# Every front-half step comes to ScalarE and VectorE one slot later than to TensorE

## The chip, the cores and the metric

The kernel runs on one core of one Trainium2 chip. The metric is device microseconds of that core for one execution of the whole program, the median of several runs. Its engines are TensorE (PE), VectorE (DVE), ScalarE (ACT), GpSimd (POOL) and the DMA queues that SyncE (SP) and POOL issue to. Each engine runs its own instruction list in order, and semaphores tie the lists together.

## The reference

One layer of a hybrid encoder is computed for 1024 prompt tokens and 64 tokens that continue a cached stream. Cut to what matters here:

```
h = rmsnorm(x)
p = h @ W_in                         # one input projection for all branches
A = gated linear attention (4 heads, blocks of 64 tokens)
B = forgetting attention (8 heads, 128 queries at a time, past of 512 for the stream)
M = cross attention into 256 memory tokens (4 heads)
x = x + W_out( sum_b sigmoid(G_b(h)) * (W_br[b] branch_b) )
h2 = rmsnorm(x)
# channel mixer: 8 heads, each picks 16 of 16384 single-neuron experts per token
for head in 8:
    e, w = top16 of product keys(h2, head)
    x += sum_e w_e * gelu(h2 . u_e) * v_e
```

## The kernel before

**Tiles and groups.** The tokens are cut into nine tiles of 128 (the last has the 64 tokens of the stream), and the tiles into four groups: tile 0, tiles 1 and 2, tiles 3 to 5, tiles 6 to 8. A group goes through a *front half*, and then its tiles go through the *experts*.

**Front half.** It is a list of steps: `in_prep` (norm and transposes), `in_unit` (a 451-column chunk of the input projection of one tile), `mix`, `fox` and `past` (the three branches, tile by tile; called mixers below; `past` prepares the caches), `gate` (gates and branch projections of the group), `out` (output projection, residual, second norm) and `sco` (scores for the picking of experts). A step has parts on several engines, which wait for one another: in a `fox` step PE makes scores in PSUM (L1151), VectorE adds the bias and takes the maximum (L1641, L1642), ScalarE exponentiates, PE transposes (L1166), ScalarE or VectorE copies (L1392, L1648), and PE multiplies by the values (L1179).

**Experts.** A token's expert is one 8 KB row that holds u_e and v_e. GpSimd gathers such rows by indirect DMA (L1847), one row for each of the 128 tokens, into a slot of a ring of eight. Two gathers make a *pair*; there are 544 pairs. For a pair VectorE makes two dot products (L1768), ScalarE the gelu and the weights and a diagonal matrix (`weigh`: L1448, L1451, L1456), and PE multiplies the diagonal with the v half (`pair`, L1284). For tiles 0 to 5 VectorE takes the second of the two value products from PE (L1784); the row for pair n stands behind the dots of pair n+1. On each head's first four pairs VectorE also does a piece of the picking of the next head's experts. The ring holds four pairs. GpSimd gathers three pairs ahead, and the gather of pair n+4 waits until PE's product of pair n and VectorE's of pair n are done.

**The order.** `make_plan` spreads the front steps of the next group over the pairs of this one. Its answer, PLAN, is a list of slots, each with one expert pair and the front steps beside it; the first group's front half stands alone at the start, the last group's pairs alone at the end. PE and SP go through a slot with `walk`: front steps first, then the pair. GpSimd gathers once a slot. ScalarE and VectorE use `trail`: the pair first, then what is left over from the slot before, then the steps of this slot. Before the change `trail` leaves `in_unit`, `gate` and `sco` steps over for the next slot, where they come behind the next pair, and does `in_prep`, `mix`, `fox`, `past` and `out` in their own slot.

Of the kernel before, what the change touches and what calls it, by code (L numbers as in the profile page):

```python
# [478 lines left out]
def layer(nc, c, t_in, outs, dram, ctx):  # L479
# [16 lines left out]
    def flat(at, n, parts=128):  # L496
        assert at + n <= AREA
        return c.area[:parts, at:at + n]
# [55 lines left out]
    sco = [flat(A0 + 7680 + k * 512, 512) for k in range(3)]  # L554
# [117 lines left out]
    def trail(front, experts):  # L672


        left = []
        for expert, beside in PLAN:
            if expert and expert[0] in experts:
                experts[expert[0]](*expert[1:])
            for step in left:
                front[step[0]](*step[1:])  # L680
            left = []
            for step in beside:
                if step[0] in ("in_unit", "gate", "sco") and expert:
                    left.append(step)
                elif step[0] in front:
                    for old in left:
                        front[old[0]](*old[1:])
                    left = []
                    front[step[0]](*step[1:])

    def walk(front, experts, front_first):
# [602 lines left out]
    def _(act):  # L1294
# [167 lines left out]
        def pair(i, r, q):  # L1462
# [7 lines left out]
            if piece == 2:  # L1470
                soften(head)

        trail({"in_prep": in_prep, "in_unit": in_unit_, "mix": mix, "fox": fox,
               "past": past, "gate": gate, "out": out_, "sco": sco_}, {"start": start, "pair": pair})


    @block.vector
    def _(dve):
# [341 lines left out]
        def end():  # L1820
            finish(NT - 1)

        trail({"in_prep": in_prep, "in_unit": in_unit_, "mix": mix, "fox": fox,
               "past": past, "gate": gate, "out": out_, "sco": sco_}, {"start": start, "pair": pair, "end": end})

# [120 lines left out]
```

How the kernel before makes its waits and increments, by code:

```python
            def step(ins):  # L210
                n[0] += 1
                ins.then_inc(s, 1)
                pool.wait_ge(s, n[0])
# [84 lines left out]
        @block.sync  # L298
# [4 lines left out]
            def mem(k):  # L303
# [11 lines left out]
                                        (c.go_bc[:, :], t_in["gla_g_out"], GDV), (c.bf_bc[:, :], t_in["fox_b_f"], FH),  # L315
                                        (c.gq_bc[:, :], t_in["fox_g_q"], FD), (c.gk_bc[:, :], t_in["fox_g_k"], FD),
                                        (c.gm_bc[:, :], t_in["mem_g_q"], MD)):
                        sp.dma_start(dst, src if n is None else src[0:1, :].broadcast_to([128, n])).then_inc(s_par, 16)
                if k == 3:
                    sp.wait_ge(s_kn, MT)
                    sp.dma_start(outs["mem_k"].rearrange("(a p) n -> p a n", p=128), kn[:, :, :]).then_inc(s_put, 16)
                    sp.wait_ge(s_mv, MT)
# [2 lines left out]
            def store(k):  # L325
                sp.wait_ge(s_ev[k % 2], k // 2 + 1)
                dst = rw_sp[k // 4].rearrange("p (a b) -> p a b", a=DT)
                sp.dma_start(dst[:, :, (k % 4) * 128:(k % 4 + 1) * 128], rw[k % 4][:, :, :]).then_inc(s_rw[k % 4], 16)
# [1 line left out]
            def route(k):  # L330
                if k:
                    if k + 3 < 16:
                        sp.wait_ge(s_mm, k)
                        load(k + 3)
                    store(k - 1)
            walk(mem, route)
            store(15)
            sp.wait_ge(s_mkT, 1)
            sp.dma_start(mkT_sp[:, :], mkT[:, :]).then_inc(s_put, 16)
            for k in range(4):
```

## Time and profile before

| what | value |
|---|---|
| runs | 4433.03, 4438.22, 4452.79 us, median 4438.22 us |
| the profiled execution | 4445.82 us, its span 4444.1 us |
| granted TensorE clock, mean | 0.875 |
| busy PE, DVE, ACT, POOL | 76%, 63%, 36%, 27% of the span |
| HBM traffic | 334 GB/s over the span |
| front half of group 0, alone | 0 to 424 us |
| mixers of fronts 1, 2, 3 beside pairs | 543 to 735, 1321 to 1668, 2467 to 3005 us |
| gates of fronts 2, 3 | 1668 to 1935, 3005 to 3286 us |
| pairs of group 3, alone | 3603 to 4444 us |

The span runs from the first to the last instruction; the profiled execution has 1.7 us around it, and lies 7.6 us over the median. Three fronts run beside pairs, and have to be looked at stage by stage: in some stages the DMA share is near 1, in others far below.

### The profile page before, as it was taken

Reading aid. Unit: us, or ns where it says so; the run is one execution under the profiler, and the core shown is the slowest. Engines: PE = TensorE matmul, PEld = TensorE weight load, DVE = VectorE, ACT = ScalarE, POOL = GpSimd, SP = SyncE. Lnnn points to the kernel's source line nnn. Section 1 sums busy time; section 2 is a strip of 40 time slices with the busy share of each in tenths; the row PEclk is TensorE's granted clock in tenths of the full one; section 3 lists DMA queues with packets and bytes.
Section 4 is the critical chain, followed back from the end, with each engine's and each line's share of the span. In section 5 each row is a group of like instructions: output and inputs, shape, how many; then the busy total and the mean of one; then the engine's idle time right before and its main releaser. Section 6 shows DMA issues by size and latency. Waiting matters only on the chain.

```text
span 4444.1 us, 33979 instructions
## 1 busy us (share of the span) xinstructions
PE 3389.7 (76%) x10219; PEld 1759.7 (40%) x10219; DVE 2805.9 (63%) x6048; ACT 1582.2 (36%) x3679; POOL 1216.8 (27%) x1122
## 2 busy tenths in 40 slices
PE   5765965986896776989689777576978867777777
PEld 4462444842444443544234344233543322322222
DVE  1112454547656784646777788685767886676677
ACT  1111154422315563432232455253443233333333
POOL 0000211113221222322333232242323344444443
PEclk9787976997997788999889778778989989999989
DMA  7557865889996788879999897878989999999998
GB/s 239 189 200 270 333 215 196 321 319 387 364 351 238 257 306 325 339 291 352 402 387 422 310 362 283 295 285 356 413 351 370 403 414 421 418 415 421 402 373 371
DMA packets 298492, 1484.95 MB, mean 334 GB/s; under 512 B 42740, under 2 KB 112372, under 8 KB 147716
## 3 DMA queue, kind: packets, MB, share of 16 engines
q0 software_dynamic: 156672, 1140.92, 64.7%
q1 hardware_dynamic: 141636, 341.86, 21.2%
q8 instruction: 81, 1.33, 0.1%
q14 instruction: 103, 0.84, 0.0%
HBM read 1415.59 MB, written 67.08 MB: 334 GB/s over the span
## 4 chain that ended last, share of the span: by engine, by line
PE 40%; DMA 24%; DVE 18%; ACT 6%; issue 6%; POOL 2%; SPq 1%; POOLq 0%; DVEq 0%; ACTq 0%
DMA c_ring<-in_uv,l_idx 17%; PE c_p_y L1284 11%; DVE c_ring L1768 7%; PE c_PB L1016 4%; PE c_PC L1016 4%; DVE l_ysb L1784 3%; PE c_PA L1271 2%; PE c_PA L1226 2%; PE c_PB L1271 2%; PE c_PB L1226 2%; PE c_PC L1226 2%; DMA c_area<-oT_sp 2%; POOL c_ring L1847 2%; PE c_PA L1254 1%; DMA c_area<-in_w_out 1%
## 5 line engine op out<-in xcount | busy, mean ns | idle before, releaser
L1847 POOL DMA_INDIRECT c_ring<-in_uv,l_idx x1088 | 1210.0, 1112 | 3203.8 <-PE c_p_y L1284 1400.0
L1284 PE MATMUL c_p_y<-c_ring,l_diag 128*128 128x512 f32 (+1 forms) x2816 | 1510.5, 676 | 451.5 <-ACT l_diag L1456 444.3
L1768 DVE CUSTOM_DVE_ANT_0 c_ring<-c_ring,l_h_cur 128x1024 f32<-128x1024 f32 x1088 | 1302.8, 1221 | 365.1 <-DMA c_ring<-in_uv,l_idx 356.6
L1284 PEld LDWEIGHTS c_p_y<-c_ring,l_diag 128*128 128x128 f32 (+1 forms) x2816 | 551.0, 207 | 1237.6 <-ACT l_diag L1456 650.9
L1448 ACT ACTIVATE l_gel<-l_dots 128x2 f32<-128x2 f32 x544 | 110.7, 203 | 1606.2 <-DVE l_dots L1768 1604.9
L1784 DVE SCALAR_TENSOR_TENSOR l_ysb<-c_ring,l_wgt,l_ysb 128x1024 f32<-128x1024 f32 x384 | 492.4, 1282 | 0.0
L1448 ACT ACT_TABLE_LOAD x207 | 265.6, 1283 | 60.0 <-DVE l_dots L1768 56.6
L1451 ACT ACTIVATE l_wgt<-l_gel,l_gw 128x1 f32<-128x1 f32 x1088 | 261.2, 287 | 17.9
L1456 ACT ACTIVATE l_diag<-c_ident,l_wgt 128x128 f32<-128x128 f32 x640 | 243.1, 399 | 16.7
L1016 PE MATMUL c_PB<-c_area 128*128 128x451 f32 (+1 forms) x576 | 228.4, 550 | 1.9 <-ACT c_area L1317 1.2
L1016 PE MATMUL c_PC<-c_area 128*128 128x451 f32 (+1 forms) x576 | 226.4, 546 | 4.3 <-DMA c_area<-in_w_in 4.3
L1226 PE MATMUL c_PA<-c_area 128*128 128x128 f32 (+3 forms) x512 | 132.1, 415 | 115.8 <-DMA c_area<-oT_sp 113.5
L1016 PEld LDWEIGHTS c_PB<-c_area 128*128 128x128 f32 (+1 forms) x576 | 107.1, 187 | 122.8 <-issue 119.0
L1226 PEld LDWEIGHTS c_PA<-c_area 128*128 128x128 f32 x512 | 93.5, 203 | 155.2 <-issue 126.0
L1016 PEld LDWEIGHTS c_PC<-c_area 128*128 128x128 f32 (+1 forms) x576 | 105.9, 185 | 123.7 <-issue 117.2
L1668 DVE TENSOR_TENSOR c_area<-c_area,c_PA 128x128 f32<-128x128 f32 (+3 forms) x32 | 14.0, 438 | 205.8 <-ACT c_area L1405 205.8
L1166 PE MATMUL c_PC<-c_ident,c_area 128*128 128x128 f32 (+2 forms) x328 | 66.4, 318 | 98.7 <-ACT c_area L1392 54.2
L1271 PE MATMUL c_PA<-c_area 128*128 128x512 f32 (+1 forms) x288 | 130.3, 607 | 1.9 <-ACT c_area L1414 1.9
L1271 PE MATMUL c_PB<-c_area 128*128 128x512 f32 (+1 forms) x288 | 128.3, 599 | 2.5 <-DMA c_area<-rw_sp 2.5
L1226 PE MATMUL c_PB<-c_area 128*128 128x128 f32 (+3 forms) x512 | 123.8, 395 | 0.0
L1226 PE MATMUL c_PC<-c_area 128*128 128x128 f32 (+3 forms) x512 | 122.9, 393 | 0.0
L1254 PE MATMUL c_PA<-c_area 128*128 128x512 f32 (+1 forms) x192 | 91.3, 632 | 24.9 <-DMA c_area<-in_w_out 21.8
(284 smaller groups left out, 3679.4 us busy)
## 6 DMA issues: line engine op xcount, KB each, us to landing
c_area<-in_w_gb SPq DMA_DIRECT2D x32, 2304.0 KB, 10.0
c_area<-in_w_in SPq DMA_DIRECT2D x32, 1804.0 KB, 9.2
c_area<-rw_sp SPq DMA_DIRECT2D x16, 2048.0 KB, 10.8
c_ring<-in_uv,l_idx POOLq DMA_INDIRECT x1088, 10.1
c_area<-in_w_out SPq DMA_DIRECT2D x8, 2048.0 KB, 9.7
proj<-c_area SPq DMA_DIRECT2D x64, 225.5 KB, 7.1
c_area<-proj SPq DMA_DIRECT2D x8, 1288.0 KB, 6.0
c_ring<-in_w_qT SPq DMA_DIRECT2D x16, 512.0 KB, 7.6
```

The lines of the kernel that those rows point to most:

```text
L1016: ins = mm_(banks[2 + u % 4][:T, :PW], hT_in[:, dt, j * 128:j * 128 + T], w[:, dt * PW:(dt + 1) * PW], start=dt == 0, stop=dt == DT - 1)
L1166: ins = tr_(PC[:widths[b], (b % 4) * 128:(b % 4) * 128 + T], prob[h % 2][:T, b * 128:b * 128 + widths[b]], c.ident[:T, :T])
L1226: mm_(ps[:, 0:N], w[:, at:at + 128], g_hT[:, e, 0:N], start=e == 0, stop=e == DT - 1)
L1254: ins = mm_((PA, PB)[j % 2][:T, half * 512:(half + 1) * 512], mixT[:, dt, j * 128:j * 128 + T], w[:, dt * 512:(dt + 1) * 512], start=dt == ...
L1271: ins = mm_(banks[v % 4][:T, :], hT_out[:, dt, j * 128:j * 128 + T], w[:, dt * 512:(dt + 1) * 512], start=dt == 0, stop=dt == DT - 1)
L1284: ins = mm_(p_y[:T, e * 512:(e + 1) * 512], diag[:, j, :T], ring[:, j, D + e * 512:D + (e + 1) * 512], start=r == 0 and q == 0 and k == 0, ...
L1448: a_(gel[:, c0:c0 + PAIR], dots[:, c0:c0 + PAIR], ACT.Gelu).then_inc(s_ae, 1)
L1451: ins = nc.scalar.mul(wgt[:, c0 + k:c0 + k + 1], gel[:, c0 + k:c0 + k + 1], gw[:, head % 3, c0 + k:c0 + k + 1])
L1456: ins = nc.scalar.mul(diag[:, (n * PAIR + k) % RING, :T], unit[:, :T], wgt[:, c0 + k:c0 + k + 1])
L1768: ins = nc.vector.tensor_tensor_reduce(out=ring[:, j, 0:D], in0=ring[:, j, 0:D], in1=h_cur[i % 2][:, :], scale=1.0, scalar=0.0, op0=ALU.mu ...
L1784: nc.vector.scalar_tensor_tensor(out=y[:T, :], in0=ring[:T, j, D:2 * D], scalar=wgt[:T, col:col + 1], in1=y[:T, :], op0=ALU.mult, op1=ALU. ...
L1847: nc.gpsimd.indirect_dma_start(out=ring[:, j, :], out_offset=None, in_=t_in["uv"][:, :], in_offset=bass.IndirectOffsetOnAxis(ap=idx[:, hea ...
```

## The change

`trail` now leaves every step that has a pair in its slot over for the next slot. So on ScalarE and VectorE `in_prep`, `mix`, `fox`, `past` and `out` come behind the next pair, as `in_unit`, `gate` and `sco` did before. The lists of PE, SP and GpSimd are the same as before, and so are the numbers of instructions of VectorE; ScalarE's list has one activation-table load less. After line 686 the lines of the changed kernel have numbers lower by 2.

```diff
             for step in left:
-                front[step[0]](*step[1:])
+                if step[0] in front:
+                    front[step[0]](*step[1:])
             left = []
             for step in beside:
-                if step[0] in ("in_unit", "gate", "sco") and expert:
+                if expert:
                     left.append(step)
                 elif step[0] in front:
-                    for old in left:
-                        front[old[0]](*old[1:])
-                    left = []
                     front[step[0]](*step[1:])
```

VectorE where the projection of front 2 ends and its mixers begin, before the change. L1515 copies the last projected chunk out of PSUM, L1537 to L1543 are the first mixer step (`mix`), L1768 the two dots of a pair, and L1784 the value product.

```order
L1515 COPY c_area<-c_PC 128x451
L1537 TENSOR_REDUCE l_st<-c_area 128x16
L1538 TENSOR_REDUCE l_st<-c_area 128x4
L1541 TENSOR_TENSOR c_area<-c_area,c_bf_bc 128x8
L1542 MEMSET c_area 128x8
L1543 MEMSET c_area 128x8
L1768 ISA c_ring,l_dots<-c_ring,l_h_cur 128x1024
L1768 ISA l_dots 128x1
L1768 ISA c_ring,l_dots<-c_ring,l_h_cur 128x1024
L1768 ISA l_dots 128x1
L1784 SCALAR_TENSOR_TENSOR l_ysb<-c_ring,l_wgt,l_ysb 128x1024
```

The same place on VectorE after the change (L1728 to L1733 are a piece of the picking).

```order
L1513 COPY c_area<-c_PC 128x451
L1766 ISA c_ring,l_dots<-c_ring,l_h_cur 128x1024
L1766 ISA l_dots 128x1
L1766 ISA c_ring,l_dots<-c_ring,l_h_cur 128x1024
L1766 ISA l_dots 128x1
L1782 SCALAR_TENSOR_TENSOR l_ysb<-c_ring,l_wgt,l_ysb 128x1024
L1728 MAX l_top<-l_onehot 128x8
L1730 MAX_INDEX l_pos<-l_top,l_onehot 128x8
L1731 TENSOR_SCALAR l_posab<-l_pos 128x16
L1732 TENSOR_SCALAR l_posab<-l_pos 128x16
L1733 CAST l_posabf<-l_posab 128x32
L1535 TENSOR_REDUCE l_st<-c_area 128x16
```

A pair and its piece of the picking now stand between the last copy of the projection and the first mixer step; the mixers that follow keep that place, one pair later each.

ScalarE where the mixers of front 2 end and its gate begins, before the change. L1378 copies the finished branch outputs, L1448 to L1456 are the weighing of a pair, and L1405 is the first sigmoid of the gate.

```order
L1378 COPY c_area<-c_PA 128x512 x2
L1448 ACTIVATE l_gel<-l_dots 128x2
L1451 ACTIVATE l_wgt<-l_gel,l_gw 128x1 x2
L1456 ACTIVATE l_diag<-c_ident,l_wgt 128x128
L1378 COPY c_area<-c_PB 128x512
L1448 ACTIVATE l_gel<-l_dots 128x2
L1451 ACTIVATE l_wgt<-l_gel,l_gw 128x1 x2
L1456 ACTIVATE l_diag<-c_ident,l_wgt 128x128
L1405 ACT_TABLE_LOAD
L1405 ACTIVATE c_area<-c_PA 128x384
```

The same place on ScalarE after the change.

```order
L1446 ACTIVATE l_gel<-l_dots 128x2
L1449 ACTIVATE l_wgt<-l_gel,l_gw 128x1 x2
L1454 ACTIVATE l_diag<-c_ident,l_wgt 128x128
L1376 COPY c_area<-c_PA 128x512 x2
L1446 ACTIVATE l_gel<-l_dots 128x2
L1449 ACTIVATE l_wgt<-l_gel,l_gw 128x1 x2
L1454 ACTIVATE l_diag<-c_ident,l_wgt 128x128
L1376 COPY c_area<-c_PB 128x512
L1403 ACT_TABLE_LOAD
L1403 ACTIVATE c_area<-c_PA 128x384
```

The last copy has moved behind one more weighing, and the sigmoid follows it without a pair between, because the gate's place has not moved.

## Rows read from the trace of the kernel before

**Rows 1.** The chain of waits that ended last, by engine.

```profile
PE 40%; DMA 24%; DVE 18%; ACT 6%; issue 6%; POOL 2%; SPq 1%; POOLq 0%; DVEq 0%; ACTq 0%
```

**Rows 2.** Stages: length, busy PE, PEld, DVE, ACT, POOL, clock, DMA share, GB/s.

```profile
543.00:735.00 192.00, 131.61 (x543) 88.81 (x542) 114.22 (x251) 97.76 (x196) 28.86 (x28) 0.74 0.56 199
1321.00:1668.00 347.00, 253.53 (x1059) 160.24 (x1057) 258.71 (x550) 205.32 (x390) 73.67 (x74) 0.77 0.73 268
2126.00:2224.00 98.00, 55.46 (x91) 19.24 (x89) 75.10 (x153) 23.55 (x73) 37.71 (x32) 0.77 1.00 400
2467.00:3005.00 538.00, 367.96 (x1350) 205.17 (x1349) 412.72 (x867) 261.60 (x536) 160.35 (x136) 0.75 0.83 304
```

**Rows 3.** VectorE's waits, 2467 to 3005 us: total us, times, longest.

```profile
DVE c_PB L1641 <- PE c_PB L1151: 22.7, 7, 4.7
DVE l_st L1537 <- ACT c_area L1334: 22.3, 3, 19.3
DVE c_ring L1768 <- DMA c_ring<-in_uv,l_idx: 11.5, 7, 3.5
```

**Rows 4.** VectorE at the start of front 2's mixers: start, duration, idle before.

```profile
1329.34 0.63 DVE L1515 COPY c_area<-c_PC 128x451 f32<-128x451 f32 x1 [2.75 <-issue]
1345.84 1.22 DVE L1537 TENSOR_REDUCE l_st<-c_area 128x16 f32<-128x1024 f32 x1 [15.87 <-ACT c_area L1334]
1347.79 1.22 DVE L1768 CUSTOM_DVE_ANT_0 c_ring<-c_ring,l_h_cur 128x1024 f32<-128x1024 f32 x1
```

**Rows 5.** VectorE's waits in front 2's output projection and scores, 1935 to 2126 us.

```profile
DVE c_area L1685 <- PE c_PA L1254: 23.6, 1, 23.6
DVE c_area L1685 <- PE c_PB L1254: 11.3, 1, 11.3
```

**Rows 6.** VectorE, then SyncE's queue, where front 2's gate begins.

```profile
1668.36 1.22 DVE L1768 CUSTOM_DVE_ANT_0 c_ring<-c_ring,l_h_cur 128x1024 f32<-128x1024 f32 x1
1712.01 0.55 DVE L1668 TENSOR_TENSOR c_area<-c_area,c_PA 128x384 f32<-128x384 f32 x1 [40.07 <-ACT c_area L1405]
...
1665.24 4.19 SPq L834 DMA_DIRECT2D oT_sp<-c_area  x3
```

**Rows 7.** GpSimd's waits for a free ring slot, 2467 to 3005 us.

```profile
POOL c_ring L1847 <- DVE l_ysb L1784: 335.1, 58, 23.8
...
POOL c_ring L1847 <- PE c_p_y L1284: 17.1, 5, 5.0
```

**Rows 8.** GpSimd's waits for a free ring slot, front 2's gate, 1668 to 1935 us.

```profile
POOL c_ring L1847 <- PE c_p_y L1284: 180.9, 23, 41.8
```

**Rows 9.** The gathers of 2467 to 3005 us: issue durations, then time to landing.

```profile
L1847 POOL DMA_INDIRECT c_ring<-in_uv,l_idx x136: 932/937/8073, 2469.0 to 3002.5; - x136
...
DMA to landing us min/median/max: 5.4/8.5/13.9
```

**Rows 10.** First dots of pairs 268 to 272 on VectorE, front 3's mixers.

```profile
2774.69 1.22 DVE L1768 CUSTOM_DVE_ANT_0 c_ring<-c_ring,l_h_cur 128x1024 f32<-128x1024 f32 x1
...
2778.17 1.22 DVE L1768 CUSTOM_DVE_ANT_0 c_ring<-c_ring,l_h_cur 128x1024 f32<-128x1024 f32 x1
...
2782.28 1.21 DVE L1768 CUSTOM_DVE_ANT_0 c_ring<-c_ring,l_h_cur 128x1024 f32<-128x1024 f32 x1
...
2786.67 1.23 DVE L1768 CUSTOM_DVE_ANT_0 c_ring<-c_ring,l_h_cur 128x1024 f32<-128x1024 f32 x1
...
2791.24 1.22 DVE L1768 CUSTOM_DVE_ANT_0 c_ring<-c_ring,l_h_cur 128x1024 f32<-128x1024 f32 x1 [1.00 <-DMA c_ring<-in_uv,l_idx]
```

**Rows 11.** VectorE's waits in front 2's gate, 1668 to 1935 us.

```profile
DVE l_ysb L1795 <- PE c_p_y L1284: 4.7, 1, 4.7
DVE c_ring L1768 <- DMA c_ring<-in_uv,l_idx: 0.4, 1, 0.4
```

**Rows 12.** PE's waits for the weights of a pair, 2467 to 3005 us.

```profile
PE c_p_y L1284 <- ACT l_diag L1456: 47.5, 20, 6.0
```

**Rows 13.** The DMA queue of the gathers: packets, MB, share of 16 engines.

```profile
q0 software_dynamic: 156672, 1140.92, 64.7%
```

## The prediction

> **What bounds the kernel now.** I read the chain of waits first. It passes from engine to engine, PE 40%, DMA 24%, VectorE 18% [rows 1], so no engine is the bound throughout, and the stages have to be taken apart. Where no front half runs, 2126 to 2224 us, the DMA engines are busy 1.00 of the time and 16 pairs take 98 us [rows 2]: gathers are the bound there, and an order on VectorE changes nothing. In the mixers the DMA share is 0.56, 0.73 and 0.83 in fronts 1, 2 and 3, and no engine's busy time fills the stage: in front 3 PE has 368 and VectorE 413 of 538 us [rows 2]. A chain through both engines bounds them: a step's part on PE, its part on VectorE or ScalarE, the next step's on PE. The stages are long because work waits its turn in it; 68 pairs (136 gathers) share the 538 us, 7.9 us for a slot.
>
> VectorE's waits in front 3's mixers show what this chain leaves open [rows 3]: for fox scores only 22.7 us in 7 waits, for the first projected data of a mixer (L1537) 22.3 us with nearly all of it in one wait of 19.3, for gathers 11.5 us. Within the mixers the pair between two steps already covers most of what PE needs; the big holes lie where one kind of step gives way to another.
>
> **The steady part of the chain costs nothing.** PE goes through front step n, then pair n. Before, VectorE goes through pair n, step n, pair n+1, step n+1; after, through pair n, step n−1, pair n+1, step n. Either way exactly one pair stands on VectorE between two neighbouring front steps, and it runs while PE makes the scores for the second of them. Step n+1 on PE needs step n from VectorE and ScalarE in both orders. So the cycle has the same parts in the same order, and only its ends differ, and what hangs on when PE comes to its pair. No instruction of weight is added or removed. The price of a pair on VectorE, used below, is 75.1 us busy over 16 pairs in the stage without a front [rows 2], 4.7 us with its share of the picking.
>
> **Term 1, ends of chains.** At the start of the mixers VectorE copies the last projected chunk at 1329.34, then waits 15.87 us until 1345.84, and only after that mixer step comes the next pair at 1347.79 [rows 4]. After the change this pair stands ahead of the mixer step and goes into the hole. The hole is a round trip through stores and loads that the copy itself sets off, so the pair shortens it by its whole 4.7 us; front 3 has the same hole of 19.3 us [rows 3]. The other such place is the start of the output projection, where VectorE waits 23.6 us for PE [rows 5]. With three fronts that makes six holes, −6 × 4.7 = −28 us.
>
> At the far ends it is the reverse. Before the gate of front 2, VectorE runs a pair at 1668.36 and then stands 40.07 us until 1712.01; the store of the branch outputs that this waits for begins at 1665.24 [rows 6]. Before the change the last mixer step comes ahead of that pair, so the pair lies inside the hole. After the change the last mixer step comes behind it, its store is issued a pair later, and nothing fills the place of the pair: +4.7 us. The same holds from `out` to `sco`, where the last norm comes a pair later, and at the start of `in_prep`. Three fronts have nine such places; the in_prep of front 3 lies where the DMA engines are saturated, and one `out` of front 1 goes straight on in its slot, so I count seven: +7 × 4.7 = +33. Together +5 us. The bounds are −28 (far ends cost nothing) and +33 (near ends gain nothing).
>
> **Term 2, the lead of the ring.** GpSimd in front 3's mixers waits 335.1 us for VectorE's product and 17.1 for PE's [rows 7]: L1784 of pair n, 3.7 us into pair n+1 (two dots of 1.22 and itself), is what frees the slot. Three slots less 3.7 us then remain for the gather. After the change PE's product of pair n still stands behind front step n on PE, but that step needs step n−1 from VectorE, which now comes behind pair n there. PE's product ends about a slot later than before and becomes what frees the ring, as it is in front 2's gate, whose steps come late already: 180.9 us of waiting for PE [rows 8]. What remains is about two slots.
>
> A gather takes 5.4 to 13.9 us to land, 8.5 in the median, and the second of a pair is issued about 1.2 us after the first [rows 9]. At 7.9 us a slot, two are 15.8 us, enough for nearly all. But slots are uneven. Pairs 268 to 272 begin at 2774.69, 2778.17, 2782.28, 2786.67 and 2791.24, 3.5 to 4.6 us apart, and the last one already waits 1.00 us for its gather [rows 10]. They have no picking and only small steps. Two such slots are 8 to 9 us against 8.5 + 1.2 us and the product on PE: short by 2 to 3 us in each stretch. I count about nine such half-heads in the mixers of fronts 2 and 3; 9 × 2.2 gives +20 us.
>
> The lower bound is 0: in front 2's gate, where VectorE has been a slot late all along and PE frees the ring, VectorE waits for gathers only 0.4 us [rows 11]. I don't take it, since slots there are longer. The upper bound is +55: every pair of these stages whose gather landed with less margin than its product is delayed, taken in full, 15 to 20 us in front 2 and 31 to 35 in front 3.
>
> **A rule beside the trace.** The Trainium skill, "DMA: Bandwidth & Descriptors", section "Anatomy of one DMA — SWDGE (gpsimd) path", gives a DMA from GpSimd's queue as about 2.0 us and its bytes over 436e3 per us; 1140.92 MB in 1088 gathers [rows 13] are 1.05 MB each, hence an estimate of 4.4 us. By that a lead of two short slots would do and term 2 would be 0. The trace disagrees: the shortest gather of the stage took 5.4 us, the median 8.5 [rows 9].
>
> **Term 3, the handing over of a tile.** In front 2's gate VectorE waited 4.7 us once for PE's last product of a tile (L1795) [rows 11], because PE stands behind a front step there. At the boundary from tile 3 to tile 4, in the mixers of front 3, PE's product now comes late in the same way: +4.7, call it +5, bounds 0 and 5.
>
> **Term 4, PE's waits for pair weights.** PE waits 47.5 us in 20 waits for ScalarE's diagonal in front 3's mixers [rows 12]. After the change a pair's dots and weights come ahead of the older front step, so these waits mostly vanish. That helps only where the next step on PE, not the ring, is late by it. Matching each of these waits with what VectorE does next leaves some 3 us: −3. The bounds are 0 and −48.
>
> **The sum.** 5 + 20 + 5 − 3 = +27 us. The profiled execution took 4445.8 us, so in its frame the changed kernel takes 4473. It lies 7.6 us over the median of the runs, 4438.2; the median should be 4438.2 + 27 = 4465 us, +0.6%.
>
> **The rivals.**
>
> *The holes win.* Near ends gain in full (−28), far ends cost nothing because the DMA round trip there also waits for something older than the moved step, and the ring is never short. With term 4 this is −31: 4407 us. For it speaks the size of the holes, 15.87 and 19.3 and 23.6 us against a pair of 4.7. Against it: the pair at 1668.36 lies ahead of a hole of 40 us now [rows 6], and a hole that costs nothing to widen would need the gate's weights or another load to be what ends it. It is decided by whether the far holes get longer by less than 0.7 us each. If they grow by half a pair each, about 4425.
>
> *No change.* The ends cancel and the lead of two slots does, as in the gate with its 0.4 us of waiting [rows 11]; 4438 to 4445 us. For it speaks that gathers in the long slots land with much to spare; against it the wait of 1.00 us that a lead of three slots leaves already [rows 10].
>
> *The ring pays in full.* Each pair that is short delays its dots, with them the step behind and PE's next pair, and so the next gather; shortages add up over a half-head, and nothing in the long slots gives them back. +55 + 5 + 5 − 3 = +62: 4500 us; with the upper end of term 1 it is 4528.
>
> **How the numbers follow.** My forecast (4450 to 4490) has 0.48, no change (4430 to 4450) 0.24, the holes 0.14, the ring in full 0.14. A measurement of this kernel tells about 0.5%, 22 us, from no change; the runs of before lie within that of their median. Faster by more (under 4416) holds most of the first rival: 0.12. Slower by more (over 4460.4) holds the ring in full and somewhat over six tenths of my forecast: 0.45. Same: 0.43. For 8 in 10 the range runs from 4418, which leaves out the first rival's body, to 4515, which leaves out the ring's end; my own case alone would be 4450 to 4490.
>
> **What would show it.** In the profile of the changed kernel GpSimd's waits in the mixers should name PE's product (L1282) where they named VectorE's; VectorE's waits for gathers in front 3's mixers should grow from 11.5 to some 25 us; the waits for L1537's successor should shrink by about 4.7 each in three places, and the long wait ahead of each gate should stay near 40 us in front 2 while the store moves a pair later. The clock could make me wrong: it was granted at 0.74 to 0.77 in the mixers [rows 2], and denser work on PE may change it either way. I would also be wrong if a late gather delayed nothing, because VectorE was about to wait for PE anyway.

## The result, and the profile after

The changed kernel takes 4481.76 us (median of 4 runs, 4481.16 to 4486.55), the kernel before 4444.16 us beside it. The ratio is 1.0088, with a 95% interval of 1.0073 to 1.0103: 0.9% slower, some 39 us. The forecast was 0.6% slower. The profiled span has grown from 4444.1 to 4479.4 us, and 7.5 us of the front half that runs alone went the other way, although nothing differs there; the rest of the program takes 43 us more.

The chain of waits, by engine, has more DMA and less VectorE in it than [rows 1]:

```profile
PE 40%; DMA 27%; DVE 15%; issue 7%; ACT 6%; POOL 2%; SPq 1%; POOLq 0%; DVEq 0%; ACTq 0%
```

The stages of mixers beside pairs, cut at the same pairs as in [rows 2] (columns as there):

```profile
540.00:733.00 193.00, 131.52 (x522) 88.97 (x520) 113.78 (x250) 96.49 (x194) 31.10 (x28) 0.70 0.53 191
1329.00:1679.00 350.00, 252.85 (x1054) 161.15 (x1053) 259.40 (x551) 207.13 (x392) 85.24 (x74) 0.78 0.73 265
2485.00:3038.00 553.00, 360.14 (x1348) 207.90 (x1346) 413.26 (x864) 260.34 (x533) 163.31 (x135) 0.73 0.79 294
```

Fronts 1 and 2 are where they were; front 3's mixers went from 538 to 553 us, with the same work on VectorE (413 us) and a lower DMA share. Cut from pair 230 to pair 298 exactly, it is 543.0 and 558.3 us; those are the lengths of this stage named below. VectorE's waits there, to be held against [rows 3], and below them the row of before that [rows 3] left out, the longest of all:

```profile
DVE l_cs L1516 <- PE c_PC L1020: 34.5, 4, 12.8
DVE c_ring L1766 <- DMA c_ring<-in_uv,l_idx: 31.7, 24, 4.5
DVE c_PB L1639 <- PE c_PB L1149: 19.6, 7, 3.8
DVE l_st L1535 <- ACT c_area L1332: 14.4, 3, 11.5
```

```profile
DVE l_cs L1518 <- PE c_PC L1022: 28.8, 4, 18.4
```

Three rows moved. The wait for gathers has gone from 11.5 us in 7 waits to 31.7 in 24. The wait at the start of a tile's mixers has gone from 22.3 to 14.4, and that for PE's L1020 (L1022 before) from 28.8 to 34.5. GpSimd's waits for a free slot in the same stretch say why the gathers are late:

```profile
POOL c_ring L1845 <- PE c_p_y L1282: 336.6, 46, 22.6
POOL c_ring L1845 <- issue: 31.8, 80, 5.5
POOL c_ring L1845 <- DVE l_ysb L1782: 21.6, 9, 5.0
```

In [rows 7] VectorE's product had 335.1 us and PE's 17.1; they have changed places. The gathers themselves take what they took in [rows 9]:

```profile
DMA to landing us min/median/max: 5.4/8.5/13.3
```

One case, first dots of pairs 268 to 272 again (compare [rows 10]; of pair 271 both dots are shown), then what ScalarE, PE and GpSimd did meanwhile. The diagonal of weights at 2788.34 and the product that starts at 2800.39 are those of pair 267, whose dots were at 2785.0; the gather at 2804.39 is for pair 271:

```profile
2791.71 1.21 DVE L1766 CUSTOM_DVE_ANT_0 c_ring<-c_ring,l_h_cur 128x1024 f32<-128x1024 f32 x1
...
2798.54 1.21 DVE L1766 CUSTOM_DVE_ANT_0 c_ring<-c_ring,l_h_cur 128x1024 f32<-128x1024 f32 x1
...
2802.03 1.22 DVE L1766 CUSTOM_DVE_ANT_0 c_ring<-c_ring,l_h_cur 128x1024 f32<-128x1024 f32 x1
...
2809.81 1.22 DVE L1766 CUSTOM_DVE_ANT_0 c_ring<-c_ring,l_h_cur 128x1024 f32<-128x1024 f32 x1 [1.80 <-DMA c_ring<-in_uv,l_idx]
2813.80 1.22 DVE L1766 CUSTOM_DVE_ANT_0 c_ring<-c_ring,l_h_cur 128x1024 f32<-128x1024 f32 x1 [2.75 <-DMA c_ring<-in_uv,l_idx]
2816.99 1.27 DVE L1766 CUSTOM_DVE_ANT_0 c_ring<-c_ring,l_h_cur 128x1024 f32<-128x1024 f32 x1
```

```profile
2788.34 0.40 ACT L1454 ACTIVATE l_diag<-c_ident,l_wgt 128x128 f32<-128x128 f32 x1
...
2797.08 3.52 PE L1177 MATMUL c_PC<-l_V,c_area 128*128 128x64 f32 x16
...
2800.39 3.73 PE L1282 MATMUL c_p_y<-c_ring,l_diag 128*128 128x512 f32 x4
...
2804.39 0.93 POOL L1845 DMA_INDIRECT c_ring<-in_uv,l_idx  x1 [12.46 <-PE c_p_y L1282]
```

The weights were ready at 2788.74, but the product stood behind a fox step's matmuls, and came 15 us after its dots. GpSimd had waited 12.46 us for it. Pair 271 then waited 1.80 and 2.75 us for its two gathers. The five pairs' first dots take 25.3 us from first to last, where they took 16.6. Over the 68 pairs of the stage the product starts 13.4 us after the pair's first dots in the median, where it started 4.8 us after them before.

At the start of front 2's mixers the pair has gone into the hole, as the order says; the wait of 15.87 in [rows 4] is 12.06:

```profile
1337.41 0.63 DVE L1513 COPY c_area<-c_PC 128x451 f32<-128x451 f32 x1 [2.74 <-issue]
1337.96 1.21 DVE L1766 CUSTOM_DVE_ANT_0 c_ring<-c_ring,l_h_cur 128x1024 f32<-128x1024 f32 x1
...
1354.96 1.22 DVE L1535 TENSOR_REDUCE l_st<-c_area 128x16 f32<-128x1024 f32 x1 [12.06 <-ACT c_area L1332]
```

Before the gate of front 2 no pair lies in the hole any more. The row in [rows 6] joins three stores; what the gate waits for last is the third. It began at 1668.92, half a us after the dots of the pair at 1668.36. Now the third begins at 1684.19, 5.4 us after the dots of the same pair at 1678.79: a pair later, as the prediction has it. The wait is 42.06 us after 40.07:

```profile
1668.92 0.51 SPq L834 DMA_DIRECT2D oT_sp<-c_area  x1
```

```profile
1684.19 0.51 SPq L832 DMA_DIRECT2D oT_sp<-c_area  x1
```

```profile
1725.77 0.56 DVE L1666 TENSOR_TENSOR c_area<-c_area,c_PA 128x384 f32<-128x384 f32 x1 [42.06 <-ACT c_area L1403]
```

### The profile page after: what moved, and what is told of

Same layout as the page of the kernel before. It is cut to its first block, busy times and chain, and to the rows that moved or that the text cites. A ratio compares the mean times of both kernels' runs of the same rounds, so it can differ in the third digit from the quotient of the medians.

```text
span 4479.4 us, 33978 instructions
## 1 busy us (share of the span) xinstructions
PE 3399.4 (76%) x10219; PEld 1770.0 (40%) x10219; DVE 2807.2 (63%) x6048; ACT 1580.0 (35%) x3678; POOL 1232.7 (28%) x1122
## 3 DMA queue, kind: packets, MB, share of 16 engines
q1 hardware_dynamic: 141636, 341.86, 20.9%
## 4 chain that ended last, share of the span: by engine, by line
PE 40%; DMA 27%; DVE 15%; issue 7%; ACT 6%; POOL 2%; SPq 1%; POOLq 0%; DVEq 0%; ACTq 0%
DMA c_ring<-in_uv,l_idx 20%; PE c_p_y L1282 11%; DVE c_ring L1766 5%; PE c_PB L1014 4%; PE c_PC L1014 4%; DVE l_ysb L1782 3%; PE c_PA L1269 2%; POOL c_ring L1845 2%; PE c_PA L1224 2%; PE c_PB L1224 2%; PE c_PC L1224 2%; PE c_PB L1269 2%; DMA c_area<-oT_sp 2%; PE c_PA L1252 1%; DMA c_area<-in_w_out 1%
## 5 line engine op out<-in xcount | busy, mean ns | idle before, releaser
L1845 POOL DMA_INDIRECT c_ring<-in_uv,l_idx x1088 | 1225.9, 1127 | 3223.2 <-PE c_p_y L1282 2122.5
L1269 PE MATMUL c_PA<-c_area 128*128 128x512 f32 (+1 forms) x288 | 133.6, 619 | 5.2 <-ACT c_area L1412 5.2
L1164 PEld LDWEIGHTS c_PC<-c_ident,c_area 128*128 128x128 f32 (+2 forms) x328 | 47.5, 174 | 201.5 <-issue 100.0
```

Source lines behind the costliest of these rows:

```text
L1164: ins = tr_(PC[:widths[b], (b % 4) * 128:(b % 4) * 128 + T], prob[h % 2][:T, b * 128:b * 128 + widths[b]], c.ident[:T, :T])
L1269: ins = mm_(banks[v % 4][:T, :], hT_out[:, dt, j * 128:j * 128 + T], w[:, dt * 512:(dt + 1) * 512], start=dt == 0, stop=dt == DT - 1)
L1845: nc.gpsimd.indirect_dma_start(out=ring[:, j, :], out_offset=None, in_=t_in["uv"][:, :], in_offset=bass.IndirectOffsetOnAxis(ap=idx[:, hea ...
```

## The experiments

The theory was that PE's product of a pair, which now stands behind a late front step, frees the ring too late. The rivals were that the ends of the chains cost, that the chain of steps itself got longer, and that the holes win.

**One part of the change at a time.** Three kernels start from the kernel before and leave one more kind of step over:

```diff
-                if step[0] in ("in_unit", "gate", "sco") and expert:
+                if step[0] in ("in_prep", "in_unit", "gate", "sco") and expert:                # e1
+                if step[0] in ("in_unit", "mix", "fox", "past", "gate", "sco") and expert:     # e2
+                if step[0] in ("in_unit", "gate", "out", "sco") and expert:                    # e3
```

> Only in_prep is left over for the next slot in addition to in_unit, gate and sco. If the way into a front costs a pair each time (the changed kernel's stretches from the first pair of a group to the start of its mixers were 4.7, 5.5 and 4.0 us longer), this takes about 13 us more than before. If that shift is given back where the projection ends and the mixers begin, it takes 0 to 4 us more.

Measured: ratio 1.0036 (1.0023 to 1.0049), 16 us slower. From the first pair of a group to the start of its mixers the three fronts took 4.3, 5.7 and 3.3 us longer. VectorE's waits at front 2's projection were 28.8 us for PE's c_PB and are now

```profile
DVE c_area L1517 <- PE c_PB L1018: 33.6, 5, 9.3
```

A pair, near enough, in each front, and front 3 pays it too.

> Only mix, fox and past are left over in addition. If the ring's lead is the main cost, VectorE's waits for gathers in front 3's mixers rise to about 30 us from 11.5 and the time by 20 to 25 us. If the chain of steps itself has become longer, the time rises as much but the waits for gathers stay near 12. If the cost lies at the ends only, the time rises by under 8 us.

Measured: ratio 1.0062 (1.0040 to 1.0084), 27 us slower; front 3's mixers 566.7 us, and in them

```profile
DVE c_ring L1770 <- DMA c_ring<-in_uv,l_idx: 33.8, 21, 4.3
...
POOL c_ring L1849 <- PE c_p_y L1286: 333.2, 46, 22.9
```

The ring's forecast, waits of about 30 us and 20 to 25 us of time, fits. That of the ends alone does not, and neither does that of a longer chain, by which the waits for gathers would have stayed near 12.

> Only out is left over in addition. Its hole at the start gains a pair (4.7 us) in each front and the way to sco loses one: 0, within 6 us either way. If the holes gain in full and the far ends cost nothing, 14 us less than before.

Measured: ratio 0.9970 (0.9951 to 0.9989), 13 us faster. The time is that of holes which gain in full and far ends which cost nothing, but the stages show something else. Cut at the same pairs, `out` gained 4.2 and 4.9 us in fronts 1 and 2, about a pair each, and 9.4 in front 3, two pairs; the way through `sco` lost 4.8 in fronts 1 and 2 and nothing in front 3. Front 3's waits for the output projection, 19.4 and 7.1 us for PE and 6.7 not for PE before, are

```profile
DVE c_area L1687 <- PE c_PA L1256: 14.9, 1, 14.9
...
DVE c_area L1687 <- issue: 6.0, 1, 6.0
DVE c_area L1687 <- PE c_PB L1256: 0.3, 1, 0.3
```

The three parts add up to 30 us; the change as a whole costs 39. With the intervals of the ratios the difference can't be told from nothing.

**The product ahead of the step.** The changed kernel, with PE taking the pair first in each slot (`walk(..., False)` on PE). No step is less late for it; only PE's product comes earlier.

```diff
-              "past": past, "gate": gate, "out": out_, "sco": sco_}, {"pair": pair}, True)
+              "past": past, "gate": gate, "out": out_, "sco": sco_}, {"pair": pair}, False)
```

> The changed kernel, with PE's pair ahead of the front steps of its slot instead of behind. By the ring: VectorE's waits for gathers in front 3's mixers fall from 31.7 to 12 us or less, GpSimd waits for VectorE's product there again and not for PE's, and the time falls by 20 to 25 us against the changed kernel, to about 15 us over before (what the ends cost). If the chain of steps has become longer in itself, the time stays at 38 us over before, or rises, since PE's steps now stand behind a pair's weights.

Measured: ratio 1.0183 (1.0160 to 1.0206), 81 us slower than before: the forecast of the ring was wrong for the whole. But the stages say two things. In front 3's mixers the stage fell from 558 to 523 us, 20 under before, and the product of VectorE frees the ring again:

```profile
2500.00:3023.00 523.00, 359.91 (x1363) 202.89 (x1361) 417.39 (x879) 262.84 (x540) 170.80 (x139) 0.78 0.86 316
```

```profile
DVE c_ring L1766 <- DMA c_ring<-in_uv,l_idx: 12.3, 7, 4.1
...
POOL c_ring L1845 <- DVE l_ysb L1782: 303.6, 54, 21.2
...
POOL c_ring L1845 <- PE c_p_y L1282: 23.3, 7, 5.8
```

From front 3's gate to the start of the pairs that run alone it lost 53 us, and front 2's gate 28. PE's pairs, now ahead of the gate steps, wait there for their weights (in front 3's gate 43.1 us in 12 waits, 15.5 in 9 in the changed kernel), and VectorE for the gate:

```profile
DVE c_area L1666 <- ACT c_area L1403: 131.5, 24, 36.0
```

So the next kernel takes the pair first only in slots whose steps are all `mix`, `fox` or `past`:

```diff
+            first = front_first
+            if front_first == "but mixers":
+                first = not all(step[0] in ("mix", "fox", "past") for step in beside)
-            if not front_first and expert and expert[0] in experts:
+            if not first and expert and expert[0] in experts:
...
-              "past": past, "gate": gate, "out": out_, "sco": sco_}, {"pair": pair}, True)
+              "past": past, "gate": gate, "out": out_, "sco": sco_}, {"pair": pair}, "but mixers")
```

> The changed kernel, with PE's pair ahead of the front steps only in slots whose steps are all mixers; gates, out, sco and the projection keep the order of the changed kernel. By the ring: the mixers of front 3 take about 523 us as they did with the pair first everywhere (558 in the changed kernel), the gates lose nothing, and the time is within 8 us of before. If what the run with the pair first everywhere showed in the mixers came from the other stages, the time stays near 38 us over before.

Measured: ratio 0.9978 (0.9962 to 0.9994), 10 us faster than before, 2 more than the 8 expected, and 1.10% or 49 us faster than the changed kernel. Front 3's mixers take 529.0 us, the product starts 4.8 us after its pair's first dots in the median, as before, and

```profile
DVE c_ring L1769 <- DMA c_ring<-in_uv,l_idx: 10.8, 9, 3.5
```

This is the run that decides: every step is as late as in the changed kernel, the dots, the gathers and their sizes are the same, and moving PE's product ahead of the step takes away the whole loss. It shows that the place of PE's product costs, not that all of it goes through the ring; the next runs part the two.

> The kernel before, with PE's pair ahead of the front steps in slots of mixers alone, and nothing late that was not. Here PE's front step stands behind weights that VectorE and ScalarE make only in the same slot (two dots of 1.22, gelu, weights and diagonal, about 4 us, and the product of 1.4 to 2.7), while VectorE then waits for that front step. If the late order is what hides this, the mixers get 4 to 6 us longer in each of about 118 slots, 300 us or more in all; if PE has room for it anyway, under 50 us.

Measured: one run, 4842.42 us, 402 us slower. That is the case in which the late order hides the wait, with 3.5 us for each of 115 slots in place of 4 to 6. Front 3's mixers took 767 us:

```profile
2636.00:3403.00 767.00, 428.11 (x1354) 228.06 (x1353) 418.43 (x878) 265.43 (x540) 138.15 (x137) 0.67 0.59 215
```

```profile
DVE c_area L1651 <- PE c_PC L1169: 74.8, 20, 7.6
DVE c_PA L1644 <- PE c_PA L1154: 61.5, 12, 7.0
DVE c_PB L1644 <- PE c_PB L1154: 39.2, 10, 6.8
```

The two orders belong together: late steps on VectorE want the pair first on PE, and steps in their own slot want it last. The granted clock in front 3's mixers was lower here, 0.67 after 0.75, and PE's busy time there rose from 368 to 428 us, so a part of the loss may be the clock's.

**Smaller gathers.** Three kernels gather 4 KB in place of 8, half of another row for each token, and do not load the v half of a slot:

```diff
-                    out=ring[:, j, :], out_offset=None, in_=t_in["uv"][:, :],
+                    out=ring[:, j, :] if n < RING // PAIR else ring[:, j, 0:D], out_offset=None,
+                    in_=t_in["uv"][:, :] if n < RING // PAIR else t_in["uv"].rearrange("n (a d) -> (n a) d", a=2),
```

> The kernel before, with half of each gathered row (4 KB instead of 8, of other rows; the v half keeps what the first four pairs brought). It is the measure for the next run: the waits for gathers in front 3's mixers should go from 11.5 us to about 0, and the stages without a front should get much shorter, since VectorE needs 4.7 us for a pair there and the gathers 6.

> The changed kernel with the same half rows. If the mixers of front 3 lost their 15 us to gathers that land too late, they lose nothing now: the stage is within 4 us of that of the run before this one, VectorE's waits for gathers there are under 3 us, and the whole is at most 10 us longer (the way into the fronts 13 to 16 more, out 13 less, the rest of the ends 5). If the late steps lengthen the chain of steps themselves, the difference of 38 us stays.

> The run with PE's pair ahead of mixer steps (all steps late), with the half rows of the two runs before. With whole rows it took 50 us less than the changed kernel, 29 of them in front 3's mixers, 21 of those in VectorE's waits for gathers. If PE's late product costs only through gathers that land late, half rows leave it little to gain: front 3's mixers within 8 us of the changed kernel's with half rows, and the whole at most 20 us less than that. If PE's late product lengthens the chain otherwise, some 50 us remain.

Measured: 4147.49, 4177.27 and 4147.50 us in this order (ratios to before 0.9338, 0.9413 and 0.9324, each within 0.0023). Front 3's mixers, and VectorE's waits for gathers in them, first for the kernel before, then the changed one, then the one with the pair first:

```profile
2396.00:2908.00 512.00, 364.24 (x1359) 204.59 (x1358) 416.68 (x877) 263.15 (x541) 170.73 (x137) 0.78 0.59 184
...
DVE c_ring L1768 <- DMA c_ring<-in_uv,l_idx: 5.2, 3, 4.0
```

```profile
2418.00:2936.00 518.00, 356.96 (x1350) 206.80 (x1348) 418.32 (x879) 262.86 (x542) 176.76 (x137) 0.75 0.56 181
...
DVE c_ring L1766 <- DMA c_ring<-in_uv,l_idx: 13.6, 12, 3.2
...
DMA to landing us min/median/max: 4.1/5.6/12.2
```

```profile
2408.00:2917.00 509.00, 354.66 (x1352) 199.56 (x1350) 416.38 (x878) 262.36 (x539) 178.08 (x138) 0.78 0.57 184
...
DVE c_ring L1769 <- DMA c_ring<-in_uv,l_idx: 7.4, 5, 4.0
```

With shorter gathers the stage loses 5.0 us to the change in place of 15.3 (cut at the pairs), and what the pair first gives back there is 7.8 in place of 29.3. That is the ring's mark in this stage. It is not a clean one: the other transfers get quicker with the gathers (the wait at the start of a tile's mixers is 12.8 us in the first of the three kernels, 22.3 with whole rows). The expectations that the gathers would hardly be waited for were wrong (5.2 and 13.6 us): the median fell to 5.6 us, the longest still took 12.2. For the whole, 30 us by the medians (33 and 40 by the ratios) between the changed kernel and either other one is more than the 10 and 20 expected, and not far below the 39 and 49 with whole rows: a good part of the loss does not hang on the length of the gathers. Part of it is the way into the fronts (4.0, 7.7 and 7.0 us longer here than in the kernel before with half rows); another part is at the gates, below.

**The versions put together.**

> As the run before this one, and in_prep is done in its own slot again, as before the change. The parts that were run apart add up to: in_prep alone cost 16 us, out alone gained 13, and the mixers should gain some 10 to 20 once the ring is freed early. So 10 to 25 us less than before, and some 13 less than with in_prep late.

Its edit is that of e5 with `step[0] != "in_prep" and expert` in `trail`. Measured: 4416.85 us, ratio 0.9944 (0.9926 to 0.9962), 25 us faster than before, at the edge of what was expected, and 65 us faster than the changed kernel. Front 3's mixers:

```profile
2459.00:2986.00 527.00, 356.12 (x1351) 200.38 (x1350) 418.33 (x880) 263.03 (x541) 172.28 (x139) 0.77 0.85 316
```

> As the fastest run so far (late steps, in_prep in its own slot, PE's pair ahead of mixer steps), but with PE's pair ahead only in front 3's mixers, behind the steps in fronts 1 and 2. In fronts 1 and 2 the gathers of the changed kernel waited for little (4.8 us more in front 2), and front 2's mixers were 12 us longer with the pair ahead than in the kernel with late in_prep alone. If that is the order, front 2's mixers come back to about 350 us and the whole gains 5 to 8 us; if those 12 us are the spread of this stage, nothing changes by more than 4.

Its edit adds `and step[1] in (-1, 6, 7, 8)` to the condition on mixers. That sets PE's pair behind the steps in fronts 1 and 2, and also, which I had not meant, in five slots of front 3: pairs 272 to 276, whose `past` steps carry the numbers 0 to 3. Measured: ratio 0.9983 (0.9971 to 0.9995), 17 us slower than the run above, not faster. Front 2's mixers did get 6 us shorter, but the stretches from the gates of fronts 1 and 2 to the next group got 8.2 and 6.6 us longer. VectorE's waits for front 1's gate, in the run above and then in this one (the longest, last in the row, is the one before the gate):

```profile
DVE c_area L1669 <- ACT c_area L1406: 82.4, 17, 31.5
```

```profile
DVE c_area L1669 <- ACT c_area L1406: 92.6, 18, 39.2
```

Front 3's mixers got 10.6 us longer, 8.8 of them between pairs 270 and 280, around the five slots; there the product of pair 273 comes 32.5 us after its first dots, 23.0 in the run above. How far one profile spreads where the order is the same shows in front 2's mixers: 347.2 us before, 346.7 with `in_prep` late and 356.3 with `out` late. Of the 12 us that I had read as a cost of the order, most can be such spread.

## Why the prediction was nearly right, and where its sizes were off

The time came out at +39 us where I had +27, in the profiles +43. All profiles can be cut at the same pairs. The changes below are sums over the three fronts, next to the forecast's share of each stage; the last column is the same change with half rows.

| stage | forecast | whole rows | half rows |
|---|---|---|---|
| way into the fronts, to the first mixer | +9.4 | +14.1 | +18.7 |
| mixers: their starts −14.1, terms 2 to 4 +22 | +7.9 | +18.2 | −7.2 |
| gates | +14.1 | +17.6 | +18.2 |
| `out` | −14.1 | −18.8 | −20.1 |
| `sco`, to the next group | +9.4 | +11.0 | +11.2 |
| pairs alone | 0 | +0.9 | −5.3 |

Each entry is from one profile on either side. In the mixers 11 of the 25 us between the columns are front 1's, where VectorE waits for no gather in any of the four kernels; they are not the ring's. The half rows' column adds up to 15.5 where the medians differ by 30: the profiled execution was the slowest of its four for the kernel before, and the fastest of its four for the changed one.

**The steady chain.** It costs little in itself: with the ring freed early, all steps late, front 3's mixers take 529.0 us, under the 543.0 of before.

**Term 2, the ring.** The mechanism is shown: who frees the ring, how late, and that moving that one thing takes the loss away. PE's product came 8.6 us later after its dots in front 3's mixers (13.4 after 4.8, in the median), "about a slot" as I had it. The size was about right too. VectorE's waits for gathers grew by 20.2 us in front 3's mixers and by 3.8 in front 2's (0.7 to 4.5), 24 in all against +20; with half rows these two stages lose 3.2 us in place of 17.7, which would give 14.5 to the gathers. The way of counting was not right: I had looked for the shortage only in half-heads with four short slots, 9 times, and there were 24 and 5 waits in the two stages, most of them under 2 us.

What the pair first gives back, 49 us, is more than this term. In front 3's mixers it is 29.3 us, twice what the change cost there, of which waits for gathers are 20.9 (31.7 less 10.8). About 16 us are at the gates. VectorE's longest wait before the gate is 38.9, 42.1 and 34.3 us in the three fronts of the changed kernel, and 32.2, 38.1 and 29.2 with the pair first. With half rows all waits for the gate still fall by 6.8 and 4.7 us in fronts 1 and 2 (103.2 to 96.4 and 100.6 to 95.9), so there it is not the length of the gathers. That PE's order among the mixers does it is shown by the last run: with the pair behind again in fronts 1 and 2 the waits are 39.2 and 41.3 us, after 31.5 and 38.1; in front 3, where the last mixer slots keep their order, 30.5 after 29.3. By what way it does it is open: from the last store to SyncE's next load it takes 9.7 and 10.9 us in the changed kernel, 3.7 and 7.1 with the pair first. The rest of the 49 us lies in `out` and `sco`, and how much of it is spread no run tells.

**Term 1, the ends.** I had +5. Without the starts of the mixers, which no stage holds alone, the ends are +24 where I had +19, and +28 with half rows. Single ends did not keep to one pair each. `in_prep` cost 16 where I counted 9, because the front that I had left out for its busy DMA engines pays as well. `out` by itself gave 13 where I had 5, since front 3's hole gained two pairs. Of the far ends to `sco`, front 1, which I had left out, and front 2 each lost a pair (VectorE's wait for PE there 12.1 to 16.8 and 8.1 to 12.8 us), and front 3, which I had counted, nothing: two errors that cancel, which is luck. At the start of the mixers front 2's hole shrank by 3.8 us and front 3's three by 7.9, and front 1's did not shrink (11.5 to 13.8).

So the terms had the right signs and about the right sizes, and the sum fell some 12 us short, spread over the mixers and the ends.

**Term 3** was 5 and the wait is 1.4 us in front 3's mixers. **Term 4**: the waits of 47.5 us [rows 12] are gone from the stage, and PE's idle time in it rose by 22 us all the same; what PE no longer waits for weights it waits for front steps. That they were worth next to nothing was right.

**The rule beside the trace.** By the Trainium skill, "DMA: Bandwidth & Descriptors", section "Anatomy of one DMA — SWDGE (gpsimd) path", a gather of 0.52 MB would be an estimate of 3.2 us, 1.2 less than a whole one. The trace disagrees: the median fell from 8.5 to 5.6 us, by 2.9. And the ring term, 0 by that rule, came out at 15 to 24 us.

Of the rivals, "the holes win" is out, since the far ends at the gates and at `in_prep` cost about a pair each; no change is out by the ratio's interval. "The ring pays in full" is right in that the shortages were spread over the stage, and too large in its 55 us. The granted clock was lower in front 3's mixers (0.73, before 0.75), but PE's busy time there fell by 8 us, and in the whole execution it rose by 10 (3389.7 to 3399.4), so the clock can't be the main cost.

## What to carry to other kernels

When work is moved a slot later on some engines, ask which instruction frees each buffer afterwards, and what stands ahead of it on its own engine. An engine whose order the change doesn't touch can become the one that frees late, and it is there that the order has to follow. Ends of chains can be priced by one pair each, with both signs, but each one has to be looked at; and a shortage in a ring falls in more and smaller waits than a count of the tightest places finds. And what a counter-change gives back is not the size of the cause it was meant for: it has to be split by stages first.

## What the runs showed of the hardware that was not expected

Halving the bytes of a gather in 128 rows took its median in front 3's mixers from 8.5 to 5.6 us, and the shortest from 5.4 to 4.1, with the DMA engines 0.56 busy in place of 0.79; the longest still took 12.2 us after 13.3. The size of a gather accounts for more of its median than of its longest time.
